# The opening norm of a hybrid decoder layer: lead weights loaded in two halves between the token tiles, two tiles scaled before any copy, meta rows summed in one pass and scaled by ACT

## The chip, the core and the metric

One NeuronCore of a Trainium2 chip runs the whole program. TensorE (PE) multiplies, with its weight loads shown as PEld; VectorE (DVE), ScalarE (ACT) and GpSimd (POOL) do elementwise work; SyncE (SP) issues most of the DMAs. The metric is the device time of one execution in microseconds (us); smaller is better.

## What is computed

One decoder layer on 16 learned meta rows followed by 512 token rows of 1024 features, float32 throughout. Only its first step is touched: the root-mean-square norm of all 528 rows, and the order in which the first weights of the input projection arrive.

```python
def rms_norm(x, g, eps=NORM_EPS):
    y = xf * lax.rsqrt(jnp.mean(xf * xf, axis=-1, keepdims=True) + eps)
    return (y * g.astype(jnp.float32)).astype(x.dtype)
...
meta = jnp.broadcast_to(meta_tokens[None].astype(x.dtype), (B, N_META, D_MODEL))
h = jnp.concatenate([meta, x], axis=1)
...
u = n @ w_in                                   # n = rms_norm(h, norm1_g)
u_shift = token_shift(u[..., :SHIFT_W], rwkv_mu)
```

After it come three mixers (a recurrent one, two kinds of attention), their gated sum, an output projection, a second norm and a mixture of 16 experts. None of that is changed.

## The kernel before

**Tiling.** The tokens are four tiles of 128 rows (t = 0 to 3) in `h`, the meta rows are a tile of 16 rows in `metax`. The projection needs the normed rows transposed: `nT` holds 8 chunks of 128 features by 528 rows, the first 16 columns for the meta rows. For a token tile ACT squares and sums the rows (L695, an accumulating pass with its own read-out), takes Ln and Exp (L699, L700) for the inverse root, DVE multiplies the tile by it into `xs` (L998), PE turns the eight 128x128 blocks into PSUM (`turned`, L1448), and DVE multiplies by the gain while it copies PSUM to `nT` (`chunks_out`, L988). Of the last tile ACT copies the upper four chunks (L712). For the meta rows DVE squares (L992), sums (L993) and, after ACT's root, scales (L1001); PE turns them (L1463) and DVE copies them (L1007).

**Projection.** A piece of weights is 256 columns, two `shift_half` pairs: for each 128 columns eight matmuls (one per chunk of features) for rows 0 to 263 (half 0) and eight for rows 264 to 527 (half 1), all at L1455. Half 0 needs tiles 0 and 1 and the meta rows, which are complete once PE may go on to the first matmul at L1455. In this trace a float32 matmul leaves two records and a transpose leaves one, so `shift_half` shows as x16, and a turn of a tile as x8.

**Order.** Every engine runs its own list in the order written, held by semaphores. PE issues matmuls of the identity into a bank that nobody reads (`unread_first`, L1439) where it would otherwise stand idle: `WARM` = 27 ahead of the first turn, 3 ahead of the turn of tile 1, 9 ahead of the first projection. They can't be cut short when data is ready earlier.

**Loads.** SP issues, in this order: tile 0 (L374), meta rows (L375), gain `g1c` as 1024 single elements (L376), tiles 1 to 3 (L378), weight piece 0 (L383, 1 MB), eight small parameter loads (L393: `muc` first, then seven others), pieces 1 and 2 (L383), and then fifteen small loads (L409). DVE's first use of a parameter (L1021) and ACT's list behind L714 wait for all eight.

Of the kernel before, what the change touches and what calls it, by code (L numbers as in the profile page):

```python
# [14 lines left out]
ALU = mybir.AluOpType  # L15
# [27 lines left out]
WARM = (27, 3, 9)  # L43
# [16 lines left out]
PARAMS_A, PARAMS_B = 16 * 8, 16 * 16  # L60
# [45 lines left out]
def hybrid_layer(nc, x, meta, g1, w_in, mu, w_up, w0, a_up, a0, k_k, k_a, r_k, ln_g, ln_b, f_b, q_g, k_g,  # L106
# [4 lines left out]
    with ExitStack() as ctx:  # L111
# [261 lines left out]
        def _(sp):  # L373
            sp.dma_start(h[:, 0, :], x[0:P, :]).then_inc(sem("tile_in0"), 16)  # L374
            sp.dma_start(metax[0:META, :], meta).then_inc(sem("meta_in"), 16)  # L375
            sp.dma_start(g1c, g1.rearrange("(c p) -> p c", p=P)).then_inc(sem("g1_in"), 16)  # L376
            for t in range(1, NT):
                sp.dma_start(h[:, t, :], x[t * P:(t + 1) * P, :]).then_inc(sem(f"tile_in{t}"), 16)  # L378
# [15 lines left out]
            for i in range(1, RING):  # L394
                load_piece(i)
# [14 lines left out]
            for i in range(RING, len(pieces)):  # L410
# [4 lines left out]
                if i == N_SHIFT:  # L415
                    sp.wait_ge(sem("xs_ready"), NT + 1)
# [264 lines left out]
        def _(act):  # L681
# [32 lines left out]
            act.wait_ge(sem("params_in"), PARAMS_A)  # L714
# [33 lines left out]
            def decay_gate(c):  # L748
                act.wait_ge(sem("wa_psum"), 2 * c + 1)
# [225 lines left out]
        def _(dve):  # L975
# [8 lines left out]
            gain = lambda c1, n: g1c[:, 0:c1].rearrange("p (c a) -> p c a", a=1).broadcast_to([P, c1, n])  # L984

            def chunks_out(t, c1):
                dve.wait_ge(sem("xT_psum"), t + 1 if t == 0 else t + 2)
                done(tt(nT[:, 0:c1, META + t * P:META + (t + 1) * P],  # L988
                        psf[:, 1024 * t:1024 * t + c1 * P].rearrange("p (c n) -> p c n", c=c1), gain(c1, P), ALU.mult), "nT_low")
# [4 lines left out]
            for t in range(NT):  # L994
                if t == 2:
                    chunks_out(1, DC)
                dve.wait_ge(sem("rstd_ready"), t + 1 if t == 0 else t + 2)
                done(ts(xs[:, t, :], h[:, t, :], stat[:, t:t + 1], None, ALU.mult), "xs_ready")  # L998
                if t == 0:
                    dve.wait_ge(sem("rstd_ready"), 2)  # L1000
                    done(ts(metax[0:META, :], metax[0:META, :], stat[0:META, 4:5], None, ALU.mult), "xs_ready")  # L1001
                    dve.wait_ge(sem("g1_in"), 16)
                if t in (1, 3):
                    chunks_out(t - 1, DC)
                if t == 1:
                    dve.wait_ge(sem("xT_psum"), 2)
                    done(tt(nT[:, :, 0:META], ps[:, 7, 0:DC * META].rearrange("p (c n) -> p c n", c=DC), gain(DC, META), ALU.mult), "nT_meta")  # L1007
            chunks_out(NT - 1, T_SPLIT)
# [5 lines left out]
            dve.wait_ge(sem("params_in"), PARAMS_A)  # L1014
# [20 lines left out]
            for n in range(3):  # L1035
                mixed(n, *(["wd_mixed"] if n == 1 else []))
# [977 lines left out]
```

## Time and profile before

| | us |
|---|---|
| median of 3 runs (812.12 to 815.58) | 812.13 |
| the profiled execution, device time | 814.37 |
| its span, first to last instruction | 812.6 |
| PE busy in the span | 793.5 |
| DVE / ACT / POOL busy | 289.6 / 207.1 / 101.3 |

The page names the engine that is busy most and the chain of work that ended last. The first 21 us, where the change lies, are read from the timeline: each row is a merged group of equal instructions with its start, its duration, its count and, in brackets, how long its engine had been idle and who released it.

### The profile page before, as it was taken

The numbers are of one execution on the slowest core, as the hardware profiler recorded it, in microseconds if no ns is written. First come the engines' busy times: TensorE is split into PE (matmuls) and PEld (weight loads), VectorE is DVE, ScalarE is ACT, GpSimd is POOL, SyncE is SP. The second block draws the span as 40 slices with busy tenths as digits, with TensorE's granted clock in tenths as the row PEclk, the third lists the DMA queues.
The fourth block names the chain that finished last, engine by engine and source line by source line (L and its number), as shares of the span: only waits on it lengthen the run. The fifth ranks groups of instructions, "written<-read, shape, count | busy, mean of one in ns | idle before, by whom it ended". The sixth has DMA issues, their size and how long they took to land.

```text
span 812.6 us, 16955 instructions
## 1 busy us (share of the span) xinstructions
PE 793.5 (98%) x7312; PEld 464.0 (57%) x7312; DVE 289.6 (36%) x547; ACT 207.1 (25%) x408; POOL 101.3 (12%) x213
## 2 busy tenths in 40 slices
PE   9999999999999899899999999999999999999995
PEld 8888888877777654455555555444444553333331
DVE  5343940033333345455544243245311442121122
ACT  4233301122253403333342122540033300111010
POOL 8850000000020100222100000000000011211211
PEclk9999999999999999999999999999999999999998
DMA  7511316300000010518111130555561389999972
GB/s 202 128 52 53 104 52 183 78 3 3 3 5 4 3 40 15 130 53 223 52 52 53 52 78 1 191 150 158 236 249 52 127 300 393 403 382 386 392 251 88
DMA packets 76154, 109.29 MB, mean 134 GB/s; under 512 B 17035, under 2 KB 61211, under 8 KB 71984
## 3 DMA queue, kind: packets, MB, share of 16 engines
q1 hardware_dynamic: 71456, 93.22, 33.7%
q0 software_dynamic: 4624, 14.99, 6.3%
q8 instruction: 58, 0.95, 0.5%
q14 instruction: 16, 0.13, 0.1%
HBM read 99.79 MB, written 10.50 MB: 136 GB/s over the span
## 4 chain that ended last, share of the span: by engine, by line
PE 96%; DVE 2%; issue 0%; ACT 0%; POOL 0%; POOLq 0%; DVEq 0%; ACTq 0%
PE ps L1561 22%; PE ps L1916 10%; PE ps L1455 9%; PE ps L1538 9%; PE ps L1849 7%; PE ps L1629 7%; PE ps L1798 6%; PE ps L1942 5%; PE ps L1543 5%; PE ps L1734 2%; PE ps L1781 2%; PE ps L1439 1%; PE ps L1765 1%; PE ps L1903 1%; PE ps L1805 1%; PE ps L1885 1%
## 5 line engine op out<-in xcount | busy, mean ns | idle before, releaser
L1561 PE MATMUL ps<-arena 128*128 128x512 f32 x304 | 142.8, 611 | 0.0
L1561 PEld LDWEIGHTS ps<-arena 128*128 128x128 f32 x304 | 55.0, 192 | 59.9 <-issue 58.7
L1916 PE MATMUL ps<-arena 128*32 128x512 f32 x624 | 84.9, 592 | 0.0
L1455 PE MATMUL ps<-arena 128*128 128x264 f32 x320 | 72.7, 386 | 0.0
L1455 PEld LDWEIGHTS ps<-arena 128*128 128x128 f32 x320 | 60.1, 189 | 11.5 <-ACT arena L762 0.7
L1629 PEld LDWEIGHTS ps<-arena 64*64 64x64 f32 x2784 | 51.3, 134 | 18.9 <-issue 13.6
L1538 PE MATMUL ps<-arena,h 128*128 128x264 f32 x256 | 61.3, 391 | 0.0
L1629 PE MATMUL ps<-arena 64*64 64x64 f32 x2784 | 56.4, 220 | 3.0 <-DVE arena L1119 2.1
L1849 PE MATMUL ps<-arena 128*128 128x512 f32 x128 | 56.0, 594 | 0.0
L1538 PEld LDWEIGHTS ps<-arena,h 128*128 128x128 f32 x256 | 47.4, 189 | 8.4
L1798 PE MATMUL ps<-yT_all,arena 128*128 128x512 f32 x112 | 50.1, 599 | 0.0
L1916 PEld LDWEIGHTS ps<-arena 128*32 128x32 f32 x624 | 22.5, 108 | 44.5 <-issue 44.5
L1942 PE MATMUL ps<-arena 128*32 128x512 f32 x384 | 43.7, 595 | 0.6 <-DVE arena L1361 0.6
L1344 DVE TENSOR_TENSOR arena<-ps,chan 128x512 f32<-128x512 f32 x24 | 15.6, 686 | 77.1 <-PE ps L1903 76.5
L1543 PE MATMUL ps<-arena 128*128 128x320 f32 (+1 forms) x128 | 40.4, 452 | 0.0
L1849 PEld LDWEIGHTS ps<-arena 128*128 128x128 f32 x128 | 23.8, 189 | 28.9 <-issue 28.9
L1211 DVE COPY arena<-ps 128x128 f32<-128x128 f32 (+3 forms) x20 | 9.8, 491 | 83.7 <-PE ps L1769 83.7
L621 POOL DMA_INDIRECT arena<-n_rows,idx x11 | 10.8, 982 | 225.1 <-DVE idx L1328 222.0
L1561 PE MATMUL ps<-arena,yT_all 128*128 128x512 f32 x80 | 38.0, 608 | 0.3 <-ACT arena L741 0.3
L1798 PEld LDWEIGHTS ps<-yT_all,arena 128*128 128x128 f32 x112 | 20.8, 190 | 25.7 <-issue 24.3
L1916 PE MATMUL ps<-yT_all,arena 128*32 128x512 f32 x144 | 35.3, 594 | 0.0
L951 ACT ACTIVATE arena<-ps 128x256 f32<-128x256 f32 x12 | 4.6, 385 | 91.2 <-PE ps L1916 91.2
(339 smaller groups left out, 977.2 us busy)
## 6 DMA issues: line engine op xcount, KB each, us to landing
arena<-in_moe_w_down SPq DMA_DIRECT2D x32, 512.0 KB, 14.0
arena<-in_moe_w_gate SPq DMA_DIRECT2D x13, 1024.0 KB, 11.2
arena<-in_moe_w_up SPq DMA_DIRECT2D x13, 1024.0 KB, 14.7
arena<-in_w_in SPq DMA_DIRECT2D x19, 512.0 KB, 3.9
arena<-in_w_in SPq DMA_DIRECT2D x5, 1024.0 KB, 5.6
h<-in_x SPq DMA_DIRECT2D x8, 512.0 KB, 5.9
arena<-in_w_out SPq DMA_DIRECT2D x1, 4096.0 KB, 12.9
h<-in_w_in SPq DMA_DIRECT2D x3, 1024.0 KB, 5.4
```

The costliest lines, as they stand in the source:

```text
L1344: v.tensor_tensor(xgT[:, s, 4 * k:4 * k + 4, :], ps[:, k, :].rearrange("p (c n) -> p c n", c=4), g2p[:, 4 * k:4 * k + 4].rearrange("p (c a ...
L1455: ins = mm(ps[:, 2 * (n % 2) + hf, 0:HALF], w[:, c, j * P:(j + 1) * P], nT[:, c, hf * HALF:(hf + 1) * HALF], start=(c == 0), stop=(c == DC ...
L1538: ins = mm(ps[:, b, 0:HALF], w[:, c, (j % 2) * P:(j % 2 + 1) * P], nT[:, c, k * HALF:(k + 1) * HALF], start=(c == 0), stop=(c == DC - 1))
L1543: ins = mm(ps[0:r, b, 0:nw], nT[:, c, k0:k0 + r], w[:, c, 0:nw], start=(c == 0), stop=(c == DC - 1))
L1561: ins = mm(ps[:, gate_bank(n), :], weights_of_gate(n)[:, c, :], nT[:, c, META:L], start=(c == 0), stop=(c == DC - 1))
L1629: return mm(ps[half(q ^ f_out), bank, c * CH:(c + 1) * CH], lhs(r, c), rhs(r, c), start=start, stop=part != "first", skip_group_check=part ...
L1734: ins = mm(psf[:, o + k0:o + k1], QK[q64, cq, qs], QK[q64, ck, k0:k1], start=True, stop=True)
L1781: ins = mm(o, V[:, k, v0:v0 + HD], pT[:, u % 2, j, k, :], start=(k == 0), stop=False, skip_group_check=True)
L1798: ins = mm(ps[:, bank(b), :], wpr[dc % 2][:, 3 * b + c, :], yT[b][:, c, :], start=(c == 0), stop=(b == 0 and c == 2), skip_group_check=(b ...
L1849: ins = mm(ps[:, out_bank(t, k), :], merged[:, c, t * P:(t + 1) * P], wout[:, c, k * 512:(k + 1) * 512], start=(c == 0), stop=(c == DC - 1))
L1916: ins = mm(ps[rs, bank, :].rearrange("p (h n) -> p h n", h=2), xgT[:, s, c, rs], w1[ws][:, :, c, :], start=(c == 0), stop=(c == DC - 1))
L1942: ins = mm(ps[rs, 4 + k, :], hT[:, s, c, rs], w2[ws][c][:, 512 * k:512 * k + 512], start=(c == 0), stop=(c == 1))
```

## The change

Six edits, all in the opening.

1. SP issues tile 1 right behind the meta rows and ahead of the gain. Piece 0 is loaded as two loads of 128 columns each, the first between the gain and tile 2 (its own semaphore `lead_in`), the second behind tile 3. Piece 1 moves ahead of all parameters, `muc` gets its own semaphore (`mu_in`), and piece 2 stays behind the parameters.
2. DVE squares and sums the meta rows with one `tensor_tensor_reduce`.
3. ACT scales the meta rows (a Copy with a scale per row), behind the sum of tile 1 and the root of the meta rows; before, that root stood between tiles 0 and 1.
4. DVE scales tiles 0 and 1 ahead of any copy, copies tile 0, the lower half of tile 1, the meta rows and the upper half of tile 1, and then scales tiles 2 and 3 and copies those.
5. PE turns the meta rows behind tile 1, issues 16, 3 and 5 unread matmuls, and cuts `shift_half(0, 0)` and `shift_half(1, 0)` in two parts of four chunks: the second part of the first waits for the upper half of tile 1, and tile 3 is turned between the two parts of the second.
6. The waits for the seven other parameters move to their first uses.

```diff
-WARM = (27, 3, 9)
+WARM = (16, 3, 5)
...
             sp.dma_start(metax[0:META, :], meta).then_inc(sem("meta_in"), 16)
+            load_tile(1)
             sp.dma_start(g1c, g1.rearrange("(c p) -> p c", p=P)).then_inc(sem("g1_in"), 16)
-            for t in range(1, NT):
-                sp.dma_start(h[:, t, :], x[t * P:(t + 1) * P, :]).then_inc(sem(f"tile_in{t}"), 16)
+            load_lead(0, sem("lead_in"))
+            load_tile(2)
+            load_tile(3)
+            load_lead(1, slot_sem(0))
...
-            load_piece(0)
+            load_piece(1)
+            sp.dma_start(muc, mu.rearrange("(c p) -> p c", p=P)).then_inc(sem("mu_in"), 16)
...
-            for i in range(1, RING):
-                load_piece(i)
+            load_piece(2)
...
                 first_norm(stat[:, t:t + 1], xs[:, t, :], h[:, t, :], P)
-                if t == 0:
+                if t == 1:
                     act.wait_ge(sem("ss_ready"), 1)
                     root(stat[0:META, 4:5], META)
+                    done(a.activation(metax[0:META, :], metax[0:META, :], ACT.Copy, scale=stat[0:META, 4:5]), "meta_scaled")
...
-            done(tt(squares, metax[0:META, :], metax[0:META, :], ALU.mult))
-            done(v.tensor_reduce(stat[0:META, 4:5], squares, mybir.AxisListType.X, ALU.add), "ss_ready")
...
+            done(v.tensor_tensor_reduce(squares, metax[0:META, :], metax[0:META, :], 1.0, 0.0, ALU.mult, ALU.add, stat[0:META, 4:5]), "ss_ready")
+            scaled(0)
+            scaled(1)
+            dve.wait_ge(sem("g1_in"), 16)
+            chunks_out(0, 0, DC)
+            chunks_out(1, 0, DC // 2)
...
+            chunks_out(1, DC // 2, DC)
+            scaled(2)
+            scaled(3)
+            chunks_out(2, 0, DC)
+            chunks_out(3, 0, T_SPLIT)
...
-            dve.wait_ge(sem("params_in"), PARAMS_A)
+            dve.wait_ge(sem("mu_in"), 16)
...
             turned(0)
-            pe.wait_ge(sem("xs_ready"), 2)
+            unread_first(WARM[1])
+            turned(1)
+            pe.wait_ge(sem("meta_scaled"), 1)
...
             unread_first(WARM[2])
-            pe.wait_ge(slot_sem(0), landed[0])
+            pe.wait_ge(sem("lead_in"), 16)
             pe.wait_ge(sem("nT_low"), 2)
             pe.wait_ge(sem("nT_meta"), 1)
-            shift_half(0, 0)
+            shift_part(0, 0, 0, DC // 2)
+            pe.wait_ge(sem("nT_low"), 3)
+            shift_part(0, 0, DC // 2, DC)
             turned(2)
+            pe.wait_ge(slot_sem(0), landed[0])
+            shift_part(1, 0, 0, DC // 2)
             turned(3)
-            shift_half(1, 0)
-            pe.wait_ge(sem("nT_low"), 4)
+            shift_part(1, 0, DC // 2, DC)
+            pe.wait_ge(sem("nT_low"), 5)
             pe.wait_ge(sem("nT_high"), 1)
```

PE's list from its first instruction. In the before kernel L1439 are the unread matmuls, L1448 turns, L1463 the meta turn, L1455 the projection:

```order
L1439 MATMUL ps<-ident 128x128 [waits ident_ready]
L1439 MATMUL ps<-ident 128x128 x26
L1448 MATMUL ps<-ident,arena 128x128 [waits xs_ready]
L1448 MATMUL ps<-ident,arena 128x128 x7
L1463 MATMUL ps<-ident,arena 128x16 [waits xs_ready]
L1463 MATMUL ps<-ident,arena 128x16 x7
L1439 MATMUL ps<-ident 128x128 x3
L1448 MATMUL ps<-ident,arena 128x128 [waits xs_ready]
L1448 MATMUL ps<-ident,arena 128x128 x7
L1439 MATMUL ps<-ident 128x128 x9
L1455 MATMUL ps<-arena 128x264 [waits nT_meta,nT_low,ring0]
L1455 MATMUL ps<-arena 128x264 x7
```

The same stretch of the changed kernel (unread matmuls L1451, turns L1460, meta turn L1481, projection L1467):

```order
L1451 MATMUL ps<-ident 128x128 [waits ident_ready]
L1451 MATMUL ps<-ident 128x128 x15
L1460 MATMUL ps<-ident,arena 128x128 [waits xs_ready]
L1460 MATMUL ps<-ident,arena 128x128 x7
L1451 MATMUL ps<-ident 128x128 x3
L1460 MATMUL ps<-ident,arena 128x128 [waits xs_ready]
L1460 MATMUL ps<-ident,arena 128x128 x7
L1481 MATMUL ps<-ident,arena 128x16 [waits meta_scaled]
L1481 MATMUL ps<-ident,arena 128x16 x7
L1451 MATMUL ps<-ident 128x128 x5
L1467 MATMUL ps<-arena 128x264 [waits nT_meta,nT_low,lead_in]
L1467 MATMUL ps<-arena 128x264 x3
```

The meta turn has moved behind the turn of tile 1, 11 and 4 of the unread matmuls are gone, and the first projection is issued four matmuls at a time.

DVE's list from the squares of the meta rows (`arena` also stands for `xs`, `metax` and `nT`; `ps` is PSUM), before:

```order
L992 TENSOR_TENSOR arena<-arena 16x1024 [waits meta_in,dve_chain]
L993 TENSOR_REDUCE stat<-arena 16x1 [waits dve_chain]
L998 TENSOR_SCALAR arena<-h,stat 128x1024 [waits rstd_ready,ss_ready]
L1001 TENSOR_SCALAR arena<-arena,stat 16x1024 [waits rstd_ready,xs_ready]
L998 TENSOR_SCALAR arena<-h,stat 128x1024 [waits rstd_ready,g1_in,xs_ready]
L988 TENSOR_TENSOR arena<-ps,chan 128x8x128 [waits xT_psum,xs_ready]
L1007 TENSOR_TENSOR arena<-ps,chan 128x8x16 [waits xT_psum,nT_low]
L988 TENSOR_TENSOR arena<-ps,chan 128x8x128 [waits xT_psum,nT_meta]
L998 TENSOR_SCALAR arena<-h,stat 128x1024 [waits rstd_ready,nT_low]
L998 TENSOR_SCALAR arena<-h,stat 128x1024 [waits rstd_ready,xs_ready]
L988 TENSOR_TENSOR arena<-ps,chan 128x8x128 [waits xT_psum,xs_ready]
L988 TENSOR_TENSOR arena<-ps,chan 128x4x128 [waits xT_psum,nT_low]
```

And changed (the two ISA rows are the one-pass sum and its read-out):

```order
L1007 ISA arena,stat<-arena 16x1024 [waits meta_in,dve_chain]
L1007 ISA stat 16x1
L1004 TENSOR_SCALAR arena<-h,stat 128x1024 [waits rstd_ready,ss_ready]
L1004 TENSOR_SCALAR arena<-h,stat 128x1024 [waits rstd_ready,xs_ready]
L999 TENSOR_TENSOR arena<-ps,chan 128x8x128 [waits xT_psum,g1_in,xs_ready]
L999 TENSOR_TENSOR arena<-ps,chan 128x4x128 [waits xT_psum,nT_low]
L1014 TENSOR_TENSOR arena<-ps,chan 128x8x16 [waits xT_psum,nT_low]
L999 TENSOR_TENSOR arena<-ps,chan 128x4x128 [waits xT_psum,nT_meta]
L1004 TENSOR_SCALAR arena<-h,stat 128x1024 [waits rstd_ready,nT_low]
L1004 TENSOR_SCALAR arena<-h,stat 128x1024 [waits rstd_ready,xs_ready]
L999 TENSOR_TENSOR arena<-ps,chan 128x8x128 [waits xT_psum,xs_ready]
L999 TENSOR_TENSOR arena<-ps,chan 128x4x128 [waits xT_psum,nT_low]
```

Scaling the meta rows has left the list, the second tile is scaled straight behind the first, and the copy of tile 1 is in two rows around the meta copy.

SP's list of DMAs, before:

```order
L374 DMA h<-in_x 128x1024
L375 DMA arena<-in_meta_tokens 16x1024
L376 DMA chan<-in_norm_g 128x8x1
L378 DMA h<-in_x 128x1024 x3
L383 DMA arena<-in_w_in 128x8x256
L393 DMA chan<-in_rwkv_mu 128x10x1
L393 DMA chan<-in_rwkv_w 128x3x1
L393 DMA chan<-in_rwkv_a 128x3x1
L393 DMA up_w<-in_rwkv_w_up 64x384
L393 DMA up_w<-in_rwkv_a_up 64x384
L393 DMA chan<-in_rwkv_k_k 128x3x1
```

And changed:

```order
L374 DMA h<-in_x 128x1024
L375 DMA arena<-in_meta_tokens 16x1024
L378 DMA h<-in_x 128x1024
L384 DMA chan<-in_norm_g 128x8x1
L382 DMA arena<-in_w_in 128x8x128
L378 DMA h<-in_x 128x1024 x2
L382 DMA arena<-in_w_in 128x8x128
L393 DMA arena<-in_w_in 128x8x256
L396 DMA chan<-in_rwkv_mu 128x10x1
L403 DMA chan<-in_rwkv_w 128x3x1
L403 DMA chan<-in_rwkv_a 128x3x1
```

Tile 1 is third, the halves of piece 0 stand on either side of tiles 2 and 3, and piece 1 precedes `in_rwkv_mu`.

## Rows read from the trace of the kernel before

**Rows 1.** Page, part 4: the chain that ended last, shares of the span by engine
```profile
PE 96%; DVE 2%; issue 0%; ACT 0%; POOL 0%; POOLq 0%; DVEq 0%; ACTq 0%
```

**Rows 2.** Timeline of PE, 0 to 17 us: start us, us, engine line op, count [idle before]
```profile
1.40 9.11 PE L1439 MATMUL ps<-ident 128*128 128x128 f32 x54 [1.40 <-POOL ident L532]
...
10.35 1.04 PE L1448 MATMUL ps<-ident,arena 128*128 128x128 f32 x8
...
11.32 0.67 PE L1463 MATMUL ps<-ident,arena 16*128 16x16 f32 x8
...
11.92 0.94 PE L1439 MATMUL ps<-ident 128*128 128x128 f32 x6
...
12.69 1.04 PE L1448 MATMUL ps<-ident,arena 128*128 128x128 f32 x8
...
13.57 2.17 PE L1439 MATMUL ps<-ident 128*128 128x128 f32 x18
...
15.58 3.73 PE L1455 MATMUL ps<-arena 128*128 128x264 f32 x16
```

**Rows 3.** Timeline of ACT and DVE in the same stretch, and ACT's four copies
```profile
5.34 1.06 ACT L695 ACTIVATE arena<-h 128x1024 f32<-128x1024 f32 x1 [3.27 <-DMA h<-in_x]
...
5.72 1.22 DVE L992 TENSOR_TENSOR arena<-arena 16x1024 f32<-16x1024 f32 x1 [3.15 <-DMA arena<-in_meta_tokens]
...
6.97 1.21 DVE L993 TENSOR_REDUCE stat<-arena 16x1 f32<-16x1024 f32 x1
...
8.21 0.76 DVE L998 TENSOR_SCALAR arena<-h,stat 128x1024 f32<-128x1024 f32 x1
8.27 0.29 ACT L699 ACTIVATE stat<-stat,chan 16x1 f32<-16x1 f32 x1 [1.23 <-DVE stat L993]
...
8.83 1.06 ACT L695 ACTIVATE arena<-h 128x1024 f32<-128x1024 f32 x1
...
10.34 0.20 ACT L700 ACTIVATE stat<-stat 128x1 f32<-128x1 f32 x1
...
10.68 0.95 DVE L998 TENSOR_SCALAR arena<-h,stat 128x1024 f32<-128x1024 f32 x1 [0.92 <-ACT stat L700]
...
12.92 0.29 DVE L1007 TENSOR_TENSOR arena<-ps,chan 128x128 f32<-128x128 f32 x1
...
13.84 1.23 DVE L988 TENSOR_TENSOR arena<-ps,chan 128x1024 f32<-128x1024 f32 x1 [0.62 <-PE ps L1448]
...
21.17 1.14 ACT L712 ACTIVATE arena<-ps,chan 128x128 f32<-128x128 f32 x4 [7.14 <-PE ps L1448]
```

**Rows 4.** Groups by shape, DVE, 400 to 510 us: shapes xcount | busy us, mean ns
```profile
L1191 DVE CUSTOM_DVE_ANT_0 arena<-ps,arena 128x528 f32<-128x528 f32 x5 | 3.5, 708 | 0.2
...
L1191 DVE DVE_READ_ACCUMULATOR2_ANT f_min<- 128x1 f32 x20 | 1.7, 83 | 0.0
```

**Rows 5.** Loads of token tiles 1 to 3 (L378), then first weight piece (L383): issue, landing
```profile
L378 SPq DMA_DIRECT2D h<-in_x x3: 432/580/912, 2.2 to 3.7; - x3
...
DMA to landing us min/median/max: 6.2/6.8/7.2
...
L383 SPq DMA_DIRECT2D arena<-in_w_in x1: 709/709/709, 4.2 to 4.2; - x1
...
DMA to landing us min/median/max: 9.8/9.8/9.8
```

**Rows 6.** Groups by shape, PE, 2 to 7 us: shapes xcount | busy us, mean ns
```profile
L1439 PE MATMUL ps<-ident 128*128 128x128 f32 x25 | 5.5, 422 | 0.0
```

**Rows 7.** PE around 330 us: timeline, then a 2 us stretch with granted clock (PEclk)
```profile
330.37 0.73 PE L1734 MATMUL ps<-arena 64*128 64x272 f32 x4 [2.13 <-DVE h L1078]
331.03 5.40 PE L1561 MATMUL ps<-arena 128*128 128x512 f32 x8
...
332.00:334.00 2.00, 2.00 (x3) 0.67 (x2) 0.46 (x1) 1.37 (x3) 0.75 (x2) 0.50 1.19 294
```

**Rows 8.** DMA from 328 to 332 us, loads of 128-column weight slices
```profile
DMA packets 2304, 1.16 MB, mean 291 GB/s; under 512 B 32, under 2 KB 2304, under 8 KB 2304
```

More of the change, by code:

```diff
@@ L375, in _, with load_tile, load_lead @@
             sp.dma_start(metax[0:META, :], meta).then_inc(sem("meta_in"), 16)
+            def load_tile(t):
+                sp.dma_start(h[:, t, :], x[t * P:(t + 1) * P, :]).then_inc(sem(f"tile_in{t}"), 16)
+            def load_lead(j, s):
+                cols = slice(j * P, (j + 1) * P)
+                sp.dma_start(slot(0)[:, :, cols], wv[:, :, pieces[0][1][0][0] + j * P:pieces[0][1][0][0] + (j + 1) * P]).then_inc(s, 16)
+            load_tile(1)
             sp.dma_start(g1c, g1.rearrange("(c p) -> p c", p=P)).then_inc(sem("g1_in"), 16)
[L377 to L378 removed]
+            load_lead(0, sem("lead_in"))
+            load_tile(2)
+            load_tile(3)
+            load_lead(1, slot_sem(0))
             def load_piece(i):
@@ L384, in load_piece @@
                     col += n
-            load_piece(0)
+            load_piece(1)
+            sp.dma_start(muc, mu.rearrange("(c p) -> p c", p=P)).then_inc(sem("mu_in"), 16)
             par = sem("params_in")
-            for dst, src in ((muc, mu.rearrange("(c p) -> p c", p=P)),
-                             (w0c, w0.rearrange("(c p) -> p c", p=P)), (a0c, a0.rearrange("(c p) -> p c", p=P)),
+            for dst, src in ((w0c, w0.rearrange("(c p) -> p c", p=P)), (a0c, a0.rearrange("(c p) -> p c", p=P)),
                              (up_w[0:64, :], w_up), (up_w[64:128, :], a_up),
@@ L983, in _ @@
                 done(v.memset(U[:, j, 0:1], 0.0))
[L984 to L989, printed above, removed]
+            gain = lambda c0, c1, n: g1c[:, c0:c1].rearrange("p (c a) -> p c a", a=1).broadcast_to([P, c1 - c0, n])
@@ new lines, in chunks_out, with scaled @@
+            def chunks_out(t, c0, c1):
+                dve.wait_ge(sem("xT_psum"), t + 1 if t < 2 else t + 2)
+                done(tt(nT[:, c0:c1, META + t * P:META + (t + 1) * P], psf[:, 1024 * t + c0 * P:1024 * t + c1 * P].rearrange("p (c n) -> p c n", c=c1 - c0),
+                        gain(c0, c1, P), ALU.mult), "nT_low")
+            def scaled(t):
+                dve.wait_ge(sem("rstd_ready"), t + 1 if t < 2 else t + 2)
+                done(ts(xs[:, t, :], h[:, t, :], stat[:, t:t + 1], None, ALU.mult), "xs_ready")
@@ L990, in _ @@
             squares = tmp_shift[0:META, :, :].rearrange("p a b -> p (a b)")[:, 0:D]
             dve.wait_ge(sem("meta_in"), 16)
-            done(tt(squares, metax[0:META, :], metax[0:META, :], ALU.mult))
-            done(v.tensor_reduce(stat[0:META, 4:5], squares, mybir.AxisListType.X, ALU.add), "ss_ready")
[L994 to L1007, printed above, removed]
@@ L1008, in _ @@
-            chunks_out(NT - 1, T_SPLIT)
+            done(v.tensor_tensor_reduce(squares, metax[0:META, :], metax[0:META, :], 1.0, 0.0, ALU.mult, ALU.add, stat[0:META, 4:5]), "ss_ready")
[4 more added lines that the diff above has]
+            chunks_out(1, 0, DC // 2)
+            dve.wait_ge(sem("xT_psum"), 3)
+            done(tt(nT[:, :, 0:META], ps[:, 7, 0:DC * META].rearrange("p (c n) -> p c n", c=DC), gain(0, DC, META), ALU.mult), "nT_meta")
@@ L1442, in turned @@
             def turned(t):
-                pe.wait_ge(sem("xs_ready"), 1 if t == 0 else t + 2)
+                pe.wait_ge(sem("xs_ready"), t + 1)
                 if t == NT - 1:
@@ L1449, in turned, with shift_part, shift_half @@
                 ins.then_inc(sem("xT_psum"), 1)
-            def shift_half(n, hf):
+            def shift_part(n, hf, c0, c1):
                 i, j = n // 2, n % 2
                 w = slot(i)
-                for c in range(DC):
+                for c in range(c0, c1):
                     ins = mm(ps[:, 2 * (n % 2) + hf, 0:HALF], w[:, c, j * P:(j + 1) * P], nT[:, c, hf * HALF:(hf + 1) * HALF],
                              start=(c == 0), stop=(c == DC - 1))
+                return ins
+            def shift_half(n, hf):
+                ins = shift_part(n, hf, 0, DC)
                 if hf == 1:
```

12 lines of the change are left out of this document (7 added, 5 removed).

## The prediction

> **What bounds the kernel now.** I read the chain that ended last first: PE holds 96% of it and DVE 2% [rows 1]. So time is won where PE's list is made shorter, or where PE stops waiting. Then I read PE's timeline of the opening [rows 2]. PE is never idle from 1.40 us on, but what it does until 15.58 is mostly the unread matmuls of L1439: 54 + 6 + 18 records. The first useful projection starts at 15.58. After it PE's list is the same multiplications in both kernels, so the change is worth what it takes off 15.58, as long as nothing later is late. Last I read ACT and DVE over the same stretch [rows 3], to see when the data that PE needs is ready, and so how much of the filling is cover and how much is surplus.
>
> Before, tile 0 lands at 5.34 and ACT has its root at about 7.04 (a tile takes ACT from 8.83 to 10.34 + 0.20 = 10.54, so 1.71). DVE is then in its two passes over the meta rows, 5.72 to 8.18, and scales tile 0 from 8.21 to 8.97. ACT waits 1.23 for the meta sum, does the meta root, and takes tile 1 only from 8.83. PE is not free before 10.35: 1.3 us of surplus filling. The copy of tile 1 ends at 13.84 + 1.23 = 15.07 and PE starts at 15.58, so here too filling overruns the data, by 0.5. Piece 0 was issued at 4.2 and landed 9.8 later, at 14.0 [rows 5]: not the last wait, but it would be if all else were 1.5 us earlier.
>
> **Part by part, in the order of PE's new list.**
>
> *First unread matmuls, 27 to 16.* In the stretch 2 to 7 us 25 records are counted, some 0.21 us from one to the next; the 18 records from 13.57 to 15.58 are 0.112 apart, half of that [rows 2, 6]. Those are TensorE at 1.2 and at 2.4 GHz. With x records at 0.213 and 54 - x at 0.11 in 10.35 - 1.40 = 8.95, x is about 29: the clock rises near 7.4. The 32 records that are left take 29 x 0.213 + 3 x 0.11 = 6.5, plus the first one's lead: the list is through at about 8.0. Is tile 0 there? The one-pass sum isn't in this stretch of the trace. Nearest is the same kind of pass at L1191: 0.708 for 528 columns, so at most 1.37 for 1024, plus 0.08 to read the sum out [rows 4]; two passes as now would be 2.43. I take 1.3, near the first, since the row is the same instruction with another shape. The sum ends at 5.72 + 1.3 = 7.0, the root is there at 7.04, DVE scales tile 0 from 7.1 to 7.9, and PE turns it at **8.0** instead of 10.35.
>
> *Tile 1.* ACT now goes on with it at 7.07 if it has landed. Before, the three tiles landed from 2.2 + 6.2 = 8.4 to 3.7 + 7.2 = 10.9, so 1.3 us apart [rows 5]; tile 0 at 5.3 and the meta rows at 5.7 to tile 1 is 2.7, of which 1.4 is over a tile's own time. Between them stood the gain, 1024 elements one by one. With the gain behind it tile 1 should land at 5.7 + 1.3 = 7.0. The bounds are 6.7 (nothing in between, a little overlap with the meta rows) and 8.4 (no help at all). I take 7.0: the surplus needs a cause, and the gain is the only load there. Root at 7.1 + 1.71 = 8.8; DVE scales it at 8.85 for 0.76 to 0.95, ready at about 9.8. PE meanwhile has turned tile 0 (0.97, from 10.35 to 11.32) and done three unread matmuls (0.77, from 11.92 to 12.69): 8.0 + 0.97 + 0.77 = 9.74. It turns tile 1 from 9.8 to 10.7 (0.88).
>
> *Meta rows.* ACT does their root at 8.8 to 9.35 (8.27 to 8.80 before) and the new scaling. No ACT Copy of that shape is in these rows; the pass over 1024 columns that is there costs 1.06, four passes over 128 columns 1.14, so 0.3 is the floor and 1.1 the likely price: ready at 10.45, hidden under the turn of tile 1. The turn of the meta rows then takes 0.60 (11.32 to 11.92): until 11.35. Queued behind ACT's scaling is tile 2.
>
> *Last filling, 9 to 5.* Ten records of 0.112: 1.15 us, until **12.5 to 12.6**. Does DVE make it? Copy of tile 0 from 9.85 to 11.1 (1.23), lower half of tile 1 at half that until 11.75, meta copy 0.29 until 12.05; the upper half until 12.7 is needed only four matmuls (1.8 us) later. It does, with 0.5 to spare.
>
> *Piece 0 in halves.* Loads of 128-column slices ran at 291 GB/s [rows 8], with the ramp of their start in that mean, so half a megabyte takes 1.8. First half: 7.0 + 1.4 (gain) + 1.8 = 10.2, needed at 12.5. Tile 2 then lands at 11.5, tile 3 at 12.8, the second half at 14.6. PE needs tile 2 scaled at 12.6 + 3.6 = 16.2; ACT can have its root at 11.5 + 1.7 = 13.2, DVE has it scaled by 14.1. The second half is needed at 17.0, tile 3 at 18.8 and scaled by 15.8. Each is covered by 2 us or more. Piece 1, twice a half, lands at 14.6 + 3.6 = 18.2 and is needed at 12.6 + 14.3 (four shift halves) + 1.8 (two turns) = 28.7. `muc` and then the other parameters queue behind it; DVE wants `muc` behind the copy of the first 128 columns, one shift half before that, at 25 or later, and the others are wanted later still. With five us and more in hand I cost all of that at nothing.
>
> *The turn of tile 3 between the parts.* ACT's four copies of its upper chunks take 1.14 [rows 3]. Before, a whole half (3.6 us) hid them; now half of one, 1.8. That is still 0.5 over 1.14 + the hand-over. Nothing, but the cover is thin: a copy later by 1 us would stall PE by 0.5.
>
> **Sum.** 15.58 - 12.6 = **3.0 us**, all on the path. Since the list is bound by its own matmuls at each of the three places, the bounds are tight: 3.3 if no hand-over costs anything, 2.3 with two full passes over the meta rows, 1.85 if tile 1 still lands at 8.4. Against the profiled execution it is 814.37 - 3.0 = 811.4 device time, span 812.6 - 3.0 = 809.6; that execution lies 2.2 over the median of the runs, so for the median 812.13 - 3.0 = **809.1**. The rest of the program is held by PE and its loads are released by PE's or its partners' progress, so it all moves forward together.
>
> **Rivals.**
>
> *A stretch at half clock goes (faster).* PE waits 2.13 us for DVE just ahead of 330.37, and at 332 to 334 the granted clock is 0.50, 1.2 GHz; the eight matmuls at 331.03 take 5.40 where eight in full clock (0.43 apart) take about 3.6 [rows 7]. That costs 1.8. The wait is in both kernels, but it comes 3 us earlier in the new one, and whether the clock answers to it may change. Without it: 812.1 - 3.0 - 1.8 = 807.3. Against: nothing in the change shortens the wait. The Trainium skill ("TensorE: Matmul & The Clock Gate", What's actually happening) says that activity is looked at on a grid that runs free of the kernel, so the same work may change clock at another place from run to run. If so, the 2.13 us might or might not bring the half clock; this trace shows that it did once.
>
> *More stretches at half clock (slower).* The same mechanism the other way: PE's shorter waits elsewhere, or those new ones between 8 and 10 us, bring one each. Price 1.8 each: one gives 810.9, two 812.7, three 814.5. It is slower by more than 0.5% (816.2) only from four on. The runs shown, 812.12 and 815.58, are 3.5 apart, two such stretches, so two do occur. For: the filling was there to keep PE busy and 15 of 39 go. Against: the waits I find in the new opening are 0.1 to 0.3 us.
>
> *Tile 1 is late all the same.* If the landing of tile 1 is set by its issue and not by the gain, or the sum takes two passes' time, the start is 13.3 to 13.75 and the time 809.8 to 810.3. That each us of lateness shows in full is the price of the cut filling.
>
> *The change doesn't reach the end.* If a later load, issued at a fixed time, holds PE, the 3.0 is given back: 812.1. Against: PE shows no wait for the pieces or parameters.
>
> **How the numbers follow.** Forecast as summed 0.55; half clock gone 0.17; tile 1 or the sum late 0.14; one or two more stretches 0.07; four or more 0.04; given back 0.03. About 0.5%, 4.1 us, is what a measurement of this kernel can tell from no change, so faster means under 808.1. That is the 0.17 and 0.03 of the forecast's own lower tail: 0.20. Slower is 0.04, and the rest, 0.76, is within. The range goes from 807.2 (half clock gone) to 811.0 (one more stretch), and leaves out some 0.12. So the likeliest result is a real gain of 0.37% that is too small to be called one.
>
> **What would show it.** In the new profile: the first turn at about 8.0, DVE's one-pass row near 1.3 us in place of 2.43; ACT's pass over tile 1 at 7.1 and not 8.8; the turn of tile 1 at 9.8, of the meta rows at 10.7; the first projection at 12.6 with no wait for `lead_in` or `nT_meta`; the second part at 14.4; no wait ahead of the first matmul for rows 264 on, near 21.5; all later groups 3 us earlier. An idle PE of over 0.5 us before 22 us, a projection that starts after 13.3, or a clock row that differs after 300 us would show the forecast wrong, and by which rival.

## The result: the opening won what was forecast, and the kernel is slower

The changed kernel takes 819.4 us (median of 8 runs, 817.25 to 821.46), the kernel before 814.36 in the 8 runs taken with it (812.12 to 815.58). The ratio is 1.0066, 95% interval 1.0051 to 1.008: slower, clear of noise, where 809.1 and a small gain had been forecast. (A ratio is taken over all runs of the two kernels and is not the quotient of their medians.) The profiled execution has this span and this chain (page, first line and part 4):

```profile
span 818.5 us, 16899 instructions
...
PE 93%; DVE 2%; DMA 1%; issue 1%; SPq 1%; ACT 1%; POOL 0%; DVEq 0%; POOLq 0%; ACTq 0%
```

PE's share of the chain fell from the 96% of [rows 1] to 93%, and DMA and issue have 1% each beside it. The opening isn't where that comes from. PE's timeline of the changed kernel, columns as in [rows 2]:

```profile
7.95 1.04 PE L1460 MATMUL ps<-ident,arena 128*128 128x128 f32 x8
...
8.83 0.83 PE L1451 MATMUL ps<-ident 128*128 128x128 f32 x6
...
9.83 1.09 PE L1460 MATMUL ps<-ident,arena 128*128 128x128 f32 x8 [0.17 <-DVE arena L1004]
...
10.86 0.67 PE L1481 MATMUL ps<-ident,arena 16*128 16x16 f32 x8
...
11.46 1.38 PE L1451 MATMUL ps<-ident 128*128 128x128 f32 x10
...
12.68 3.73 PE L1467 MATMUL ps<-arena 128*128 128x264 f32 x16
```

Turn of tile 0 at 7.95, of tile 1 at 9.83, of the meta rows at 10.86, first projection at 12.68 instead of the 15.58 of [rows 2]: 2.90 us earlier, 3.0 had been summed. DVE and ACT beside it, to be held against [rows 3]:

```profile
5.67 1.21 DVE L1007 CUSTOM_DVE_ANT_0 arena<-arena 16x1024 f32<-16x1024 f32 x1 [3.11 <-DMA arena<-in_meta_tokens]
...
6.82 0.07 DVE L1007 DVE_READ_ACCUMULATOR2_ANT stat<- 16x1 f32 x1
...
7.21 1.06 ACT L704 ACTIVATE arena<-h 128x1024 f32<-128x1024 f32 x1 [0.27 <-DMA h<-in_x]
...
9.02 0.75 DVE L1004 TENSOR_SCALAR arena<-h,stat 128x1024 f32<-128x1024 f32 x1 [1.23 <-ACT stat L709]
...
9.51 1.15 ACT L716 ACTIVATE arena<-arena,stat 16x1024 f32<-16x1024 f32 x1
...
12.12 0.69 DVE L999 TENSOR_TENSOR arena<-ps,chan 128x512 f32<-128x512 f32 x1
```

The one-pass sum is 1.21 + 0.07 (1.3 was taken), ACT starts tile 1 at 7.21 (7.1), its scaling of the meta rows costs 1.15 (1.1). Tile 1 and the first half of piece 0, issue and landing as in [rows 5]:

```profile
L378 SPq DMA_DIRECT2D h<-in_x x1: 414/414/414, 1.7 to 1.7; - x1
...
DMA to landing us min/median/max: 5.4/5.4/5.4
```

```profile
L382 SPq DMA_DIRECT2D arena<-in_w_in x1: 582/582/582, 2.6 to 2.6; - x1
...
DMA to landing us min/median/max: 6.4/6.4/6.4
```

Tile 1 landed at 1.7 + 5.4 = 7.1 and the first half at 2.6 + 6.4 = 9.0, 1.2 us sooner than summed.

So some 8.8 us were lost later (818.5 - 812.6 + 2.9). I laid the starts of the same PE instructions of both profiles over each other, and cut the program where the steps are. The 64x64 stage is the recurrent mixer's chain of 64x64 products (L1629 before, L1651 after), with a few wide projection matmuls between them.

| stretch, us | before | changed | 
|---|---|---|
| start to first projection | 15.6 | 12.7 |
| projection, to the first 64x64 product | 154.2 | 154.2 |
| 64x64 stage | 120.3 | **127.9** |
| from there to the attention's first turns | 46.2 | 46.1 |
| attention | 183.4 | 183.4 |
| branch projections | 56.5 | **57.7** |
| rest | 236.5 | 236.6 |

7.6 of the 8.8 are in one stage, which the diff doesn't touch, and 1.2 in the branch projections. In that stage PE's costliest group, from 165 to 295 us (xcount | busy us, mean ns | idle just before, and for whom), before and changed:

```profile
L1629 PE MATMUL ps<-arena 64*64 64x64 f32 x2784 | 56.4, 220 | 3.0 <-DVE arena L1119 2.1 <-ACT arena L821 0.8
```

```profile
L1651 PE MATMUL ps<-arena 64*64 64x64 f32 x2784 | 59.2, 221 | 7.7 <-issue 5.0 <-DVE arena L1131 1.8 <-ACT arena L832 0.8
```

The same 2784 matmuls are busy 2.8 us longer and stand 4.7 longer; the new idle time, 5.0, is put down to "issue": no engine and no load is waited for. It comes in single stalls in the middle of rows of equal matmuls with no semaphore between them. The bracket of a row counts idle time only, 0.2 to 1.0 us; from the start of one matmul to the start of the next, which takes in the last matmul's own 0.2, they are 0.4 to 1.2 us, and all nine of the stage come to 7.0 of its 7.6 (over 0.02 us a record without them). PE's timeline of the changed kernel, 179 to 200 us:

```profile
178.79 0.85 PE L1651 MATMUL ps<-arena 64*64 64x64 f32 x43
180.44 0.46 PE L1651 MATMUL ps<-arena 64*64 64x64 f32 x15 [0.81 <-issue]
...
185.03 0.81 PE L1651 MATMUL ps<-arena 64*64 64x64 f32 x38
186.46 0.68 PE L1651 MATMUL ps<-arena 64*64 64x64 f32 x26 [0.62 <-issue]
...
191.25 0.68 PE L1651 MATMUL ps<-arena 64*64 64x64 f32 x27
192.20 0.80 PE L1651 MATMUL ps<-arena 64*64 64x64 f32 x37 [0.28 <-issue]
...
197.13 0.46 PE L1651 MATMUL ps<-arena 64*64 64x64 f32 x16
198.30 0.93 PE L1651 MATMUL ps<-arena 64*64 64x64 f32 x48 [0.71 <-issue]
```

Counting the PE matmul records that stand before them, those four stalls come behind 1355, 1482, 1609 and 1736 records: 127 apart. With the larger ones further on (2628, 2755, 2881 and 3898; a small one at 3771) every distance is close to a multiple of 127. A record is a weight load and a matmul, so 127 records are 254 instructions, and a few waits stand among them. PE's own code is loaded over queue q8 in packets of 0.02 MB (58 packets, 0.95 MB on the page, 16 KB each). PE's queue has 14860 records in the trace of the kernel before (weight loads, matmuls, waits and branches): 256 for each of the 58 packets. The two kernels below with over 15050 have 59 packets. This is how the trace shows one, the windows 181 to 183.5 us and 183.5 to 184.5 us ahead of the stall that ends at 186.46:

```profile
DMA packets 0, 0.00 MB, mean 0 GB/s; under 512 B 0, under 2 KB 0, under 8 KB 0
```

```profile
q8 instruction: 1, 0.02, 8.0%
```

A packet started at 183.6 and the stall ended at 186.46. In the 2.5 us ahead of 183.5 no queue moved anything, so other transfers didn't hold that packet up. For the four stalls above, the last packet had started 2.4 to 2.9 us before PE went on. The Trainium skill has the mechanism ("Runtime: NRT & Kernel Launch", Instruction fetch mechanics): code comes in blocks of 256 instructions that the sequencer fetches while it executes, and crossing a block is "mostly hidden". The block size agrees with the count here; that it is hidden doesn't hold for this stage, with stalls of 0.4 to 1.2 us.

The traces of all fourteen kernels of this document, those of the experiments below included, make this exact. Count every record of PE's queue from 0. Between 160 and 300 us they show 51 "issue" stalls of over 0.15 us, and in all 51 the first instruction that is late is number 193 of a block of 256. That can't be an accident. Not every crossing stalls, though. Give each crossing the packet that its place in the count pairs it with, and take how long that packet had started before PE got there (before the end of PE's last matmul ahead of the crossing):

| packet started ahead of PE's arrival by | crossings | with a stall of over 0.15 us |
|---|---|---|
| 1.5 to 2.5 us | 67 | 51 |
| 2.5 us or more | 336 | 0 |

In all 51 PE went on 2.2 to 3.0 us after its packet had started. So a stall is a packet that started late. At the crossings of the four stalls above it had started 1.7 to 2.2 us ahead in the changed kernel, and 3.9 to 4.9 in the kernel before. It started 3.2 to 3.7 us after PE had passed the crossing ahead of it in the changed kernel and 0.3 to 1.3 in the kernel before.

### The profile page after: what moved, and what is told of

Read it like the earlier page. It is cut to its first block, busy times and chain, and to the rows that moved or that the text cites. A ratio compares the mean times of both kernels' runs of the same rounds, so it can differ in the third digit from the quotient of the medians.

```text
span 818.5 us, 16899 instructions
## 1 busy us (share of the span) xinstructions
PE 793.4 (97%) x7282; PEld 461.8 (56%) x7282; DVE 287.3 (35%) x547; ACT 208.3 (25%) x409; POOL 100.6 (12%) x213
## 4 chain that ended last, share of the span: by engine, by line
PE 93%; DVE 2%; DMA 1%; issue 1%; SPq 1%; ACT 1%; POOL 0%; DVEq 0%; POOLq 0%; ACTq 0%
PE ps L1583 21%; PE ps L1938 10%; PE ps L1467 9%; PE ps L1560 9%; PE ps L1651 7%; PE ps L1871 7%; PE ps L1820 5%; PE ps L1964 5%; PE ps L1565 5%; PE ps L1756 2%; PE ps L1803 2%; PE ps L1787 1%; PE ps L1925 1%; PE ps L1827 1%; PE ps L1907 1%
## 5 line engine op out<-in xcount | busy, mean ns | idle before, releaser
L1467 PE MATMUL ps<-arena 128*128 128x264 f32 x320 | 72.9, 386 | 0.0
L1651 PEld LDWEIGHTS ps<-arena 64*64 64x64 f32 x2784 | 52.9, 134 | 24.7 <-issue 19.4
L1651 PE MATMUL ps<-arena 64*64 64x64 f32 x2784 | 59.2, 221 | 7.7 <-issue 5.0
L1467 PEld LDWEIGHTS ps<-arena 128*128 128x128 f32 x320 | 60.0, 189 | 11.5 <-ACT arena L773 0.7
L1938 PEld LDWEIGHTS ps<-arena 128*32 128x32 f32 x624 | 22.5, 108 | 44.5 <-issue 44.5
L1356 DVE TENSOR_TENSOR arena<-ps,chan 128x512 f32<-128x512 f32 x24 | 15.6, 687 | 77.1 <-PE ps L1925 76.5
```

Of the source, the lines that this page charges most:

```text
L1356: v.tensor_tensor(xgT[:, s, 4 * k:4 * k + 4, :], ps[:, k, :].rearrange("p (c n) -> p c n", c=4), g2p[:, 4 * k:4 * k + 4].rearrange("p (c a ...
L1467: ins = mm(ps[:, 2 * (n % 2) + hf, 0:HALF], w[:, c, j * P:(j + 1) * P], nT[:, c, hf * HALF:(hf + 1) * HALF], start=(c == 0), stop=(c == DC ...
L1651: return mm(ps[half(q ^ f_out), bank, c * CH:(c + 1) * CH], lhs(r, c), rhs(r, c), start=start, stop=part != "first", skip_group_check=part ...
L1938: ins = mm(ps[rs, bank, :].rearrange("p (h n) -> p h n", h=2), xgT[:, s, c, rs], w1[ws][:, :, c, :], start=(c == 0), stop=(c == DC - 1))
```

## The experiments

**Theory A, code loading.** The change made PE's list 60 instructions shorter (15 unread float32 matmuls, each two weight loads and two matmuls) and added one. That moved every crossing behind the opening by some 30 records against the work. In the 64x64 stage PE uses code fastest: it crosses a block every 3 to 6 us there in most cases, and every 24 to 29 us in the projection. **Theory B**: one of the moved loads or scalings is late for that stage. **Theory C**: the new opening does it some other way.

The tool for it is a wait on a semaphore that has long been raised: an instruction without work. `2 * n + 1` waits ahead of a matmul give n instructions more. The counts below are of instructions added, as the traces have them.

### Length and order apart

`e1_after_pad59`:

```diff
-            unread_first(WARM[0])
+            for i_ in range(WARM[0]):
+                unread_first(1)
+                more_ = 59 * (i_ + 1) // WARM[0] - 59 * i_ // WARM[0]
+                for _ in range(2 * more_ + 1 if more_ else 0):
+                    pe.wait_ge(sem("ident_ready"), 1)
```

> The changed kernel, with 59 waits on an already raised semaphore added to PE's list between the 16 first unread matmuls (a float32 matmul is two weight loads and two matmuls, so 15 fewer matmuls took 60 instructions away; this gives them back without work). Theory A, code loading: PE stands still where its list crosses into code that has not landed yet (16 KB packets of queue q8), and the shorter list has moved these places within the 64x64 stage from 180 to 285 us. Then the opening stays at a first projection near 12.7, the 64x64 stage looks as before the change, and the time is 2 to 3 us under before, ratio near 0.997. Theory B, data: the new order of loads and scalings makes something later late in that stage; then the padding changes nothing and the ratio stays near 1.007.

Measured: 812.55 against 813.84, ratio 0.9978 (0.9964 to 0.9991), as theory A has it. The 64x64 stage took 120.5 us and has no stall of over 0.15 us; 60 instructions were added.

`e2_before_less_filling`:

```diff
-WARM = (27, 3, 9)
+WARM = (16, 3, 5)
```

> The kernel before with one edit, the unread matmuls cut from 27, 3, 9 to 16, 3, 5. Theory A (code loading): the 64x64 stage loses what the changed kernel loses there, some 8 us, though no load, scaling or copy has been touched; the opening gains 0.4 us at most, ratio 1.006 to 1.010. Theory B (data): 0.0 to 0.4 us faster than before, ratio 0.9995 to 1.0.

Measured: 820.24, ratio 1.0082 (1.0063 to 1.0101). One line, no load or scaling touched, and the stage took 126.4 us with 4.1 us of idle "issue" (same columns as above):

```profile
L1629 PE MATMUL ps<-arena 64*64 64x64 f32 x2772 | 58.6, 221 | 6.4 <-issue 4.1 <-DVE arena L1119 1.5 <-ACT arena L821 0.8
```

The stalls stand behind 1355, 1482, 1610, 1737 records and so on, within one record of those of the changed kernel. The opening gained 1.0, not 0.4: PE then waited 2.2 for tile 0 but did the later fillings sooner. It is about as slow as the changed kernel (the two intervals overlap): it has most of that kernel's loss, 6.1 of 7.6 us in the stage, and a third of its gain. Theory B has nothing left to explain here.

`e3_after_full_filling`, the reverse edit in the changed kernel:

```diff
-WARM = (16, 3, 5)
+WARM = (27, 3, 9)
```

> The changed kernel with the unread matmuls back at 27, 3, 9, so PE's list is as long as before to within two instructions. Theory A: the 64x64 stage as before the change; the opening is held by the filling, about 10.4 + 5.2 as before, so the ratio is 0.999 to 1.001. Theory B: the opening is no better than before and the later loss remains: ratio near 1.010.

Measured: 815.34, ratio 1.0015 (1.0001 to 1.0029), the stage at 121.2, the first projection at 15.4. With the old filling the reordering alone is worth 0.2 us in the opening; the cut alone (e2) is worth 1.0; both together 2.9. The excess over the 0.999 to 1.001 that was expected isn't in the opening: 0.8 us is one stall in the stage, at a crossing where the kernel before has one of 0.17, and this profile has a second stretch at half clock, from 642 us, that costs 0.5.

`e4_after_pad120` is e1 with 120 in place of 59:

```diff
-                more_ = 59 * (i_ + 1) // WARM[0] - 59 * i_ // WARM[0]
+                more_ = 120 * (i_ + 1) // WARM[0] - 120 * i_ // WARM[0]
```

> As the first, with 120 waits added instead of 59, half a code packet (256 instructions) on from the changed kernel. Theory A: another pattern of stalls in the 64x64 stage, its sum anywhere between that of before and 10 us more, unlike that of the kernel with 59; ratio 0.995 to 1.008. Theory B: no difference from the changed kernel, 1.007, unless the waits themselves hold PE, which would show as idle time ahead of 8 us.

Measured: 821.16, ratio 1.009 (1.0073 to 1.0107), outside what I gave. The stage took 121.4, so as theory A has it, but the waits themselves held PE in the opening, by more than I had thought they could:

```profile
1.41 13.14 PE L1451 MATMUL ps<-ident 128*128 128x128 f32 x32 [1.41 <-POOL ident L541]
14.78 1.94 PE L1464 MATMUL ps<-ident,arena 128*128 128x128 f32 x8 [0.24 <-issue]
```

The 32 records take 13.1 us (121 instructions were added among them), and the turn of a tile, 1.04 at full clock above, takes 1.94: TensorE was still at 1.2 GHz. The first projection started at 21.5. As a test of the stage it counts; as a time it doesn't, which is why the next ones put the waits elsewhere.

### The same waits behind the opening

In the changed kernel's `shift_part`, from the third 128 columns on (n >= 2), where a matmul takes PE long enough to hide a wait; `N` is 59, 30, 256 and 128 in the four kernels, and 61, 30, 260 and 132 instructions are added:

```diff
                 for c in range(c0, c1):
+                    if n >= 2:
+                        at_[0] += 1
+                        more_ = N * at_[0] // 128 - N * (at_[0] - 1) // 128 if at_[0] <= 128 else 0
+                        for _ in range(2 * more_ + 1 if more_ else 0):
+                            pe.wait_ge(sem("ident_ready"), 1)
                     ins = mm(ps[:, 2 * (n % 2) + hf, 0:HALF], ...
```

> The changed kernel with 61 waits on an already raised semaphore spread one at a time over PE's matmuls of the third and later 128 columns of the projection (30 to 100 us), behind the opening and ahead of the 64x64 stage. Theory A (code loading): the same cure of the 64x64 stage as with the 59 waits in the opening, and the opening keeps its first projection at 12.7; 2.5 to 3.5 us under before, and the half clock near 330 us may come or go (1.4 to 1.8). Ratio 0.995 to 0.997. Theory C: something in the opening made the difference there (its waits spaced PE's first work); then the stage still stalls: 1.006.

Measured: 812.45 against 814.66, ratio 0.9979 (0.9967 to 0.9991), a smaller gain than the 0.995 to 0.997 expected; the stage 120.8, the projection itself not longer by 0.01 us. No stall of over 0.15 us is left, and no stretch at half clock near 330:

```profile
L1658 PE MATMUL ps<-arena 64*64 64x64 f32 x2784 | 56.4, 220 | 3.3 <-DVE arena L1131 2.4 <-ACT arena L832 0.8
```

> The same with 30 waits, half the way back to the code positions of before. Theory A: the crossings fall 15 records earlier than in the changed kernel; some of its eight stalls (0.4 to 1.2 us each, 6.7 in sum) shrink, so 0.997 to 1.004. Theory C: 1.006 to 1.007, the stalls unchanged.

Measured: 816.55, ratio 1.002 (1.000 to 1.004), the stage 124.5. Five of the changed kernel's nine stalls are gone, those of 180 to 198 us among them; the others stand behind 2613, 2740, 2866 and 3756 records, 15 before 2628, 2755, 2881 and 3771. Thirty instructions are 15 records.

> The same with 260 waits, one whole code packet of 256 instructions and four more. Theory A with packets of 16 KB: the crossings fall on the same matmuls as in the changed kernel (two records off), so the stalls come back at the same places and the ratio is 1.005 to 1.008 although far more waits have been added than in the kernels that cured it. If the cure came from the waits as such, it is cured here too: 0.996.

Measured: 817.32, ratio 1.0033 (1.002 to 1.0046), the stage 124.1. Less than the 1.005 I gave at least, but this is the most telling of the four: more waits than any other, and the stalls are back. Its stalls in the second third of the stage, and then the changed kernel's:

```profile
226.66 0.45 PE L1658 MATMUL ps<-arena 64*64 64x64 f32 x12 [0.49 <-issue]
...
232.42 0.58 PE L1658 MATMUL ps<-arena 64*64 64x64 f32 x23 [0.51 <-issue]
...
238.26 0.80 PE L1658 MATMUL ps<-arena 64*64 64x64 f32 x35 [0.61 <-issue]
```

```profile
229.88 0.44 PE L1651 MATMUL ps<-arena 64*64 64x64 f32 x10 [0.49 <-issue]
...
235.35 0.57 PE L1651 MATMUL ps<-arena 64*64 64x64 f32 x21 [0.17 <-issue]
...
241.46 0.70 PE L1651 MATMUL ps<-arena 64*64 64x64 f32 x33 [0.90 <-issue]
```

They stand behind 2626, 2753 and 2879 records, two before those of the changed kernel, and so do the two later ones, behind 3769 and 3896: 260 instructions are one packet of 256 and four more, and four are two records. The four stalls of 180 to 198 us didn't come back, so a crossing at the same work need not stall. The packets of these four had started 4.2 to 4.9 us ahead here, against 1.7 to 2.2 in the changed kernel.

> The same with 132 waits, half a code packet. Theory A: the crossings fall half way between those of the changed kernel; stalls at other places or none. The kernel with 120 waits in its opening showed few stalls in the 64x64 stage, so I expect the stage as before and the ratio 0.995 to 0.998; by theory C 1.006.

Measured: 814.83, ratio 1.0006 (0.9989 to 1.0023), above what I expected; its profiled execution has the stage at 121.5 and a span of 810.4, which the median doesn't bear out. Its ten runs go from 812.2 to 816.5.

### The loss moved into the kernel before, and three more places

`e9_before_mid197` has the same edit in `shift_half` of the kernel before, N = 193, 197 instructions added:

```diff
                 for c in range(DC):
+                    if n >= 2:
+                        at_[0] += 1
+                        more_ = 193 * at_[0] // 128 - 193 * (at_[0] - 1) // 128
+                        for _ in range(2 * more_ + 1 if more_ else 0):
+                            pe.wait_ge(sem("ident_ready"), 1)
```

> The kernel before, untouched but for 197 waits on a raised semaphore over the projection (30 to 100 us). With the 60 instructions that the changed kernel has fewer that is 257, one code packet, so crossings fall where they do in the changed kernel. Code loading: stalls of 0.4 to 1.2 us in the 64x64 stage at PE records 1385, 1512, 1639, 1766, 2657, 2785, 2911, 3928 or some of them (the changed kernel's places plus the 30 records that its list lacks), 3 to 8 us in sum, ratio 1.003 to 1.009. If the loss belonged to the changed opening, this kernel is as before, 1.000.

Measured: 821.07 against 814.33, ratio 1.009 (1.0072 to 1.0107), the stage 126.2. Stalls behind 1385, 1639, 1766, 2658, 2785, 2911 and 3928 records: seven of the eight places named beforehand, to within one record. Five of them in PE's timeline:

```profile
182.00 0.46 PE L1636 MATMUL ps<-arena 64*64 64x64 f32 x15 [0.20 <-issue]
...
193.22 0.80 PE L1636 MATMUL ps<-arena 64*64 64x64 f32 x37 [0.28 <-issue]
...
199.04 0.93 PE L1636 MATMUL ps<-arena 64*64 64x64 f32 x48 [0.43 <-issue]
...
230.11 0.44 PE L1636 MATMUL ps<-arena 64*64 64x64 f32 x10 [0.49 <-issue]
...
235.85 0.57 PE L1636 MATMUL ps<-arena 64*64 64x64 f32 x21 [0.40 <-issue]
```

The kernel before can be made as slow as the changed one by instructions that do nothing, their number worked out from the size of a packet. That rules out B and C for the loss in this stage.

`e10_after_late56` adds 56 instructions to the changed kernel behind the stage:

```diff
                     for c in range(DC):
+                        if 8 <= n < 16:
+                            for _ in range(3 if c else 1):
+                                pe.wait_ge(sem("ident_ready"), 1)
                         ins = mm(ps[:, gate_bank(n), :], weights_of_gate(n)[:, c, :], ...
```

> The changed kernel with 56 waits on a raised semaphore behind the 64x64 stage, in the gate products of 340 to 500 us. Code loading: the crossings ahead of 285 us don't move, so the 64x64 stage takes 126 to 128 us as in the changed kernel, ratio 1.005 to 1.008. If added waits help anywhere, or the length of the whole list counts, it is near 0.998.

Measured: 817.62, ratio 1.0044 (1.0026 to 1.0062), the stage 127.3: not cured, as A says. The ratio is a little under the 1.005 given; its interval includes it. The 1.1 us wait of the branch projections (below) is absent in its profile; that may be the difference, and isn't shown to be.

`e11_after_wide_filling` makes the list shorter still, by 48, without changing PE's work:

```diff
-            unread_first(WARM[0])
+            wide = ident[:].rearrange("p (a n) -> p a n", a=1).broadcast_to([P, 4, P])
+            for _ in range(WARM[0] // 4):
+                mm(ps[:, 5, :].rearrange("p (a n) -> p a n", a=4), ident[:], wide, start=True, stop=True)
```

> The changed kernel with the first 16 unread matmuls of 128 columns replaced by 4 of 512 columns, the same work for PE in 48 fewer instructions. Code loading: the crossings fall 24 records later than in the changed kernel; by the other kernels so far, which had stalls at 0, 30 and 260 instructions and few at 60 and 132, this untried side can be either, 0.996 to 1.009; any stall stands 24 records behind one of the places of the changed kernel. The opening as in the changed kernel, first projection 12.5 to 13.2.

Measured: 816.51, ratio 1.0032 (1.0016 to 1.0049), the stage 123.7, the opening 12.7. Three stalls instead of nine, behind 1609, 1736 and 3898 records. With 24 records fewer ahead of the stage, these are matmuls 24 further on in the work, as expected: the same places in the count, three of the changed kernel's own, on other work.

`e12_mid77` is e5 with N = 75:

> The changed kernel with 77 waits over the projection, between the 61 that cured the stage and the 132 that did too. Code loading: few stalls, the 64x64 stage at 120 to 121.5 us, ratio 0.996 to 0.999. If the cure at 61 was luck of one value, the stage stalls again, over 124.

Measured: 813.07, ratio 0.9985 (0.9973 to 0.9996), the stage 121.2. So the cure is no single lucky value.

| kernel | instructions against the changed one, ahead of the stage | 64x64 stage, us | ratio to before |
|---|---|---|---|
| e11 | -48 | 123.7 | 1.0032 |
| changed | 0 | 127.9 | 1.0066 |
| e6 | +30 | 124.5 | 1.0020 |
| e1 (in the opening) | +60 | 120.5 | 0.9978 |
| e5 | +61 | 120.8 | 0.9979 |
| e12 | +77 | 121.2 | 0.9985 |
| e8 | +132 | 121.5 | 1.0006 |
| e7 | +260 | 124.1 | 1.0033 |

e5 keeps the whole change and beats both kernels, as e1 and e12 do: 0.21% under before, its interval under 1, though below the 0.5% that one measurement can tell.

## Why the prediction was wrong, point by point

- **What bounds the kernel.** Right for the opening: PE's filling, data next. That PE's own list costs the same in both kernels from the first projection on was the mistake.
- **The sum of the opening, 3.0.** Right to about 0.1 in each term on the path. Measured 2.90: first turn 7.95 (8.0), one-pass sum 1.28 (1.3), tile 1 there at 7.1 (7.0), meta scaling 1.15 (1.1), first projection 12.68 (12.5 to 12.6). The gain had indeed held tile 1 back: with the gain behind it, tile 1 came 1.3 us earlier, 0.5 of it because it was issued earlier (1.7 against 2.2). The term for the first half of piece 0 was too careful by 1.2 us, and the cover of ACT's four copies held.
- **The step that failed**: "The rest of the program is held by PE and its loads are released by PE's or its partners' progress, so it all moves forward together." I went through the data that PE waits for and not its instructions. Cutting 15 matmuls was costed as time saved only; that they also shift all later code against the packets it comes in was left out. It cost 7.6 us in this profile, two and a half times the gain. Another 2.2 us of the miss are the base: 812.13 was the median of three runs, and eight give 814.36, so the sum would have meant 811.4.
- **The rivals.** None named this. "Given back later" was the nearest, with 0.03, and had a late load in mind. The slower rival had the wrong mechanism, half clock.
- **Half clock.** The stretch near 330 us stayed in the changed kernel, as the forecast had it. Eight matmuls in 3.70 in e5 are what [rows 7] would be without it:

```profile
328.27 0.73 PE L1763 MATMUL ps<-arena 64*128 64x272 f32 x4 [2.13 <-DVE h L1090]
328.93 3.70 PE L1590 MATMUL ps<-arena 128*128 128x512 f32 x8
```

And the changed kernel at the same place, with the granted clock (PEclk, the third number from the end) at 0.50:

```profile
336.00:338.00 2.00, 2.00 (x4) 0.84 (x3) 1.12 (x3) 0.68 (x2) 0.14 (x1) 0.50 1.18 290
```

The stretch between the stage and the attention takes 44.5 in e1, e5, e8 and e11 and 46.0 to 46.2 in all others, so the half clock costs 1.6 (1.8 was worked out) and comes with the same wait, 2.13 us in both groups, or doesn't. What decides it isn't settled here. It adds to the gain of e1 and e5 in their profiles: of e5's 3.5 us (span 809.1 against 812.6), 1.7 are from there.
- **The 1.2 us of the branch projections** were not foreseen either:

```profile
PE ps L1820 <- DMA arena<-in_w_p_fox: 1.1, 1, 1.1
```

PE waits for a load of `w_p_fox` that SP issues in sequence behind others. The profile of before has no such wait, nor have those of e3, e5, e10, e11 and e12; the other seven have one of 0.2 to 0.8. e2 and e9, at 0.8, have the load order of before, so the new order alone isn't its cause. The cause is open; nothing was tried on it.
- **The chances.** 0.76 for no change and a range of 3.8 us assumed that all unknowns but the half clock were in the opening. Nothing in them allowed for another effect outside it.

Open too: what delays a code packet, and so why a crossing at the same work stalls in one kernel and not in another. What is shown is that every stall stands at one place in the instruction count modulo 256, that it comes only where the packet had started less than 2.5 us before PE got there, and that kernels with nearly the same number of instructions ahead of the stage have nearly the same late packets (changed, e2 and e10; before, e1, e3 and e5). How long the stage takes can't be told from the count modulo 256 alone: e7, four instructions from the changed kernel by that measure, takes 124.1 and not 127.9.

## What to carry to other kernels

Where one engine runs many short instructions for a long stretch, the number of instructions ahead of that stretch is a hidden parameter: removing idle filling from an opening can cost more behind than it wins. If a profile shows idle time for "issue" in rows of equal instructions, count the distance between such stalls; if it is a constant number of instructions or a multiple of one, pad the list ahead, where the engine is slow per instruction, and measure two or three lengths. And judge an edit by stage, not by the total alone: here a total of +0.7% held a stage that won all that was expected of it.

## What the runs showed of the hardware that I had not expected

- Code loading stalls PE for 0.4 to 1.2 us at a crossing, nine times in 128 us in the changed kernel. PE stood only where the packet of 16 KB had started less than 2.5 us before PE got there (51 of 67 crossings, against 0 of 336), and went on 2.2 to 3.0 us after its start.
- Waits on a raised semaphore are not free for PE: 121 instructions of them among 32 short records stretched 6.7 us to 13.1. Spread over matmuls of 0.22 us a record they cost nothing measurable, even two instructions to a matmul (e7, the projection 154.2 us as before).
- In e4 TensorE didn't rise to 2.4 GHz during those 13 us, though a matmul was always near: the turn at 14.78 still took 1.94. With the same matmuls unbroken it rose by 7.5 in the changed kernel. The Trainium skill ("TensorE: Matmul & The Clock Gate", What's actually happening) calls the slow clock the default that activity releases; the trace agrees in that; in this one profile, matmuls spaced out by waits didn't release it for 13 us.
- A one-pass multiply-and-sum on DVE over 16 rows of 1024 took 1.21 + 0.07 us, where the multiply alone had taken 1.22 [rows 3].
